# A 2-layer block on one core: the RWKV row stage, the recurrence and the layer's end get a new order of work

## The reference, cut to what matters

```python
r, k, v = jnp.einsum('nbtc,ncd->nbtd', xs[:3], w_rkv)
w_log = -jax.nn.softplus(-(w0 + jnp.tanh(xw @ w1) @ w2)) - 0.5
decay = jnp.exp(-jnp.exp(w_log))
a = jax.nn.sigmoid(a0 + (xa @ a1) @ a2)
g = jax.nn.sigmoid(xg @ g1) @ g2
kk = split(k * k_k)
kk = kk / jnp.maximum(jnp.sqrt(jnp.sum(kk * kk, axis=-1, keepdims=True)), 1e-12)
k_mod = k * (1.0 + (a - 1.0) * k_a)
# per head: S_t = S_{t-1} diag(w_t) + (S_{t-1} a_t) b_t^T + v_t k_t^T ;  y_t = S_t r_t
y = wkv7(rh, wh, kh, vh, -kk, kk * ah)
y = (y - mean) * lax.rsqrt(var + GN_EPS) * gn_g + gn_b        # per head
y = y + jnp.sum(rh * kh * r_k, axis=-1, keepdims=True) * vh   # the bonus
out = (y.reshape(B, T, C) * g) @ wo
```

## Time and profile before

| | |
|---|---|
| median of 3 runs | 1590.67 us (1590.26 to 1593.71) |
| the profiled execution | 1589.26 us, its span 1587.4 us |
| mean granted TensorE clock | 0.942 of 2.4 GHz |
| busy in the span | PE 90%, DVE 56%, ACT 44%, POOL 4% |

### The profile page before, as it was taken

How to read it: one execution, slowest core, us unless ns; L and a number is a source line. 1 busy time by engine, 2 the same in 40 slices (tenths; PEclk the granted TensorE clock), 3 DMA queues, 4 the chain that set the end, 5 groups by cost and what they waited for, 6 DMA issues and landing times.

```text
span 1587.4 us, 22472 instructions
## 1 busy us (share of the span) xinstructions
PE 1426.4 (90%) x8310; PEld 1164.7 (73%) x8310; DVE 883.2 (56%) x1246; ACT 703.2 (44%) x1125; POOL 68.3 (4%) x51
## 2 busy tenths in 40 slices
PE   6999999788979889999996798888999983899998
PEld 5888877666767778887874688857888862578887
DVE  4454567865533454455939654355555577355554
ACT  5343465453544453444444222224444463454443
POOL 0000000000000000000005003100000001000000
PEclk9999999888999999999898899969999996899999
DMA  8556556334434446465423000033555640135553
GB/s 267 185 180 210 169 163 212 106 120 146 133 105 160 123 157 213 159 196 188 134 67 118 2 3 28 19 106 117 189 184 185 201 160 27 53 123 184 192 182 113
DMA packets 145859, 221.43 MB, mean 139 GB/s; under 512 B 16844, under 2 KB 65240, under 8 KB 145656
## 3 DMA queue, kind: packets, MB, share of 16 engines
q1 hardware_dynamic: 145784, 220.40, 42.1%
HBM read 219.30 MB, written 1.05 MB: 139 GB/s over the span
## 4 chain that ended last, share of the span: by engine, by line
PE 81%; DVE 11%; ACT 5%; issue 2%; POOL 1%; DMA 1%; SPq 0%; ACTq 0%; DVEq 0%
PE acc L268 11%; PE gp L268 11%; PE acc L269 11%; PE acc L270 11%; PE gp L270 11%; PE gp L269 11%; PE tp L839 1%; DVE sb_w_lo L262 1%; PE gp L2116 1%; PE acc L2132 1%; ACT sb_arena L2604 1%; PE acc L2129 1%; PE tp L449 1%; ACT sb_xa_hi L427 1%; DVE sb_xa_lo L434 1%
## 5 line engine op out<-in xcount | busy, mean ns | idle before, releaser
L262 DVE TENSOR_TENSOR sb_w_lo<-sb_raw,sb_w_hi 128x1024 fp32r<-128x1024 f32 x400 | 479.3, 1228 | 252.5 <-ACT sb_w_hi L251 251.7
L251 ACT ACTIVATE sb_w_hi<-sb_raw 128x1024 fp32r<-128x1024 f32 x400 | 409.7, 1059 | 288.9 <-PE acc L270 150.6
L268 PE MATMUL gp<-sb_w_hi,sb_xa_hi 128*128 128x512 f32 (+1 forms) x736 | 295.8, 402 | 15.2 <-DVE sb_xa_lo L434 10.0
L270 PE MATMUL gp<-sb_w_lo,sb_xa_hi 128*128 128x512 f32 (+1 forms) x736 | 289.8, 394 | 0.0
L269 PE MATMUL gp<-sb_w_hi,sb_xa_lo 128*128 128x512 f32 (+1 forms) x736 | 289.6, 393 | 0.0
L268 PEld LDWEIGHTS gp<-sb_w_hi,sb_xa_hi 128*128 128x128 f32 x736 | 141.7, 193 | 49.7 <-issue 17.1
L270 PEld LDWEIGHTS gp<-sb_w_lo,sb_xa_hi 128*128 128x128 f32 x736 | 141.1, 192 | 30.0
L269 PEld LDWEIGHTS gp<-sb_w_hi,sb_xa_lo 128*128 128x128 f32 x736 | 141.8, 193 | 27.5
L268 PE MATMUL acc<-sb_w_hi,sb_mid_hi 128*128 128x512 f32 x408 | 159.1, 390 | 0.0
L270 PE MATMUL acc<-sb_w_lo,sb_mid_hi 128*128 128x512 f32 x408 | 158.9, 389 | 0.0
L269 PE MATMUL acc<-sb_w_hi,sb_mid_lo 128*128 128x512 f32 x408 | 158.7, 389 | 0.0
(11 more groups left out here) (371 smaller groups left out, 1848.2 us busy)
## 6 DMA issues: line engine op xcount, KB each, us to landing
sb_raw<-in_ffn_w SPq DMA_DIRECT2D x264, 256.0 KB, 4.3
sb_raw<-in_mlp_w SPq DMA_DIRECT2D x256, 256.0 KB, 2.9
sb_raw<-in_w_in SPq DMA_DIRECT2D x72, 256.0 KB, 3.5
sb_raw<-in_a_w_rkv SPq DMA_DIRECT2D x48, 256.0 KB, 3.6
sb_raw<-in_xattn_w_kv SPq DMA_DIRECT2D x32, 256.0 KB, 3.6
sb_raw<-in_w_out SPq DMA_DIRECT2D x16, 256.0 KB, 3.0
sb_raw<-in_xattn_w_q SPq DMA_DIRECT2D x16, 256.0 KB, 5.5
sb_raw<-in_xattn_w_o SPq DMA_DIRECT2D x16, 256.0 KB, 4.0
```

The costliest lines, as they stand in the source:

```text
L251: A.e.activation(w_hi[:, s], raw[:, r], ACT.Copy).then_inc(hi_done, 1)
L262: V.e.tensor_tensor(w_lo[:, s], raw[:, r], w_hi[:, s].bitcast(F32), ALU.subtract).then_inc(lo_done, 1)
L268: e.matmul(dst, xh, wh, start=start, stop=False)
L270: return e.matmul(dst, xh, wl, start=False, stop=stop)
```

## The change

- Biases: w0 and a0 become a 65th row of the second low-rank matrices, against a row of ones (read from the table `causal`), so the sigmoids read PSUM directly. The a parts move to `up_a` and `low_a`, in the memory of `mid`. k_k and k_a are loaded early, r_k after up-a.
- Order of TensorE: first half of k, g, up-w, second half of k (into `tp`), decay ends, up-a, first half of v, the sums, the sum shifted by one token as a product with the table `tri` moved by a column (`pe_sum`), token tile 0 of v's second half, the shifted sum of tile 1. Tile 1 of v's second half is done in four pieces within unit 0, whose transposes come alone.
- k*k_k, b, r and all of the head norm move from GpSimd to VectorE. GpSimd keeps the powers. kk is worked on by column halves.
- The bonus weights (`dve_weigh`) are made in iterations 1 and 2 of the recurrence, output chunks are split in iterations 1 to 4, and tile 0's norm and bonus run in iterations 5 to 7.
- Stream 1's buffers lie in the memory of `xb` and `mid`, so six output chunks are loaded before the recurrence.
- The last unit is interleaved with tile 0's gate, transposes (two groups of four k tiles, `pe_wide`) and its output product for the first 512 columns. Tile 1's norm is done in two parts, twelve heads and four. `pe_out` then does tile 1's gate, and the rest of the product by token and column half.

The diff, cut to its core and eight columns of indent taken off:

```diff
+    before = np.arange(-1, P)[None, :]
+    put("tri", -DECAY * ((s <= before).astype(np.float32) - (s < P // 2).astype(np.float32)))
...
+        mid_f = [shadow[:, x, :] for x in range(2)]
+        self.up_a, self.low_a, self.r_k = mid_f[0], mid_f[1][:, 0:256], mid_f[0]
...
+        sp.dma_start(self.up[64:65, :], a["a_w0_2"]).then_inc(self.lora2_loaded, 16)
+        sp.dma_start(self.low_w[64:65, :], self.ones()).then_inc(self.lora2_loaded, 16)
...
+        r, k, v = self.prods
+        for c in range(r.first[0], r.first[1]):
             load_chunk(sp, c)
-        self.bias(sp, 1, 0, a["a_w0_2"][0], xattn.post.freed)
-        self.bias(sp, 2, 1, a["a_a0_2"][0], ffn2_post.freed)
-        for c in range(self.prods[0].end, second):
+        sp.wait_ge(chunk_used, ffn2.end)
+        sp.dma_start(self.up_a[0:64, :], a["a_a2_2"][0]).then_inc(self.up_a_loaded, 16)
+        sp.dma_start(self.up_a[64:65, :], a["a_a0_2"]).then_inc(self.up_a_loaded, 16)
+        sp.dma_start(self.low_a[64:65, :], self.ones()).then_inc(self.up_a_loaded, 16)
+        for c in range(r.first[1], r.end):
             load_chunk(sp, c)
-        self.bias(sp, 3, 0, a["a_k_k_2"][0], (self.w_in, NT))
-        for c in range(second, self.prods[2].end):
+        sp.wait_ge(*ffn2_post.freed)
+        sp.dma_start(gain_b[1][:, :], a["a_k_k_2"][0].partition_broadcast(P)).then_inc(self.bias_loaded, 16)
+        for c in range(k.first[0], k.end):
...
+        sp.wait_ge(*xattn.post.freed)
+        sp.dma_start(gain_b[0][:, :], a["a_k_a_2"][0].partition_broadcast(P)).then_inc(self.k_a_loaded, 16)
+        for c in range(v.first[0], v.end):
+            load_chunk(sp, c)
+        sp.wait_ge(self.a_up, NT)
+        sp.wait_ge(self.bias_loaded, 16)
+        sp.dma_start(self.r_k, a["a_r_k_2"][0].rearrange("h d -> (h d)").partition_broadcast(P)).then_inc(self.bias_loaded, 16)
+        for c in range(self.out.first[0], self.out.first[0] + 6):
...
-        sp.wait_ge(self.y_done, 2 * self.GROUPS)
-        for c in range(ahead, self.out.end):
+        for c in range(self.out.first[0] + 6, self.out.end):
             load_chunk(sp, c)
...
-        self.pe_product(T, 0, XA, 4, (1,))
+        r, k, v = self.prods
+        r.pe(T, 1, XA, self.bank(1), (self.mixed_lo, 4))
         self.pe_wa(T)
-        self.pe_product(T, 1, XB, 5, (0, 1))
+        k.pe(T, 0, XB, self.bank(2), (self.mixed_lo, 5), stage(self.taken, 2))
...
+    def pe_sum(self, T, t, dst, tri, done):
+        for b in range(2):
+            mm = T.e.matmul(dst(b), tri, rows(0)[:, t, b * 512:(b + 1) * 512], start=True, stop=True)
+        mm.then_inc(*T.one(done))
...
-        T.e.wait_ge(self.lora2_loaded, 32)
-        T.e.wait_ge(self.low, 4)
+        r, k, v = self.prods
+        T.e.wait_ge(self.lora2_loaded, 48)
+        T.e.wait_ge(*stage(self.taken, 4))
+        self.pe_up_rows(T, self.low_w, self.up, self.w_up)
+        k.pe(T, 1, XB, self.bank(3), (self.mixed_lo, 5), (self.low, 4))
+        T.e.wait_ge(self.w_sig, NT)
         T.e.wait_ge(*stage(self.taken, 6))
-        self.pe_up_rows(T, 0, self.w_up)
-        self.prods[2].pe(T, 0, XA, self.bank(4), (self.mixed_lo, 6), stage(self.taken, 8))
-        T.e.wait_ge(self.w_in, NT)
-        self.pe_up_rows(T, 1, self.a_up)
-        self.prods[2].pe(T, 1, XA, self.bank(5), (self.mixed_lo, 6), stage(self.taken, 10))
-        T.e.wait_ge(self.a_in, NT)
-        T.e.wait_ge(self.w_sig, NT)
-        for t in range(NT):
-            for b in range(2):
-                mm = T.e.matmul(acc[:, t, b * 512:(b + 1) * 512], const("tri"), rows(0)[:, t, b * 512:(b + 1) * 512], start=True, stop=True)
-            mm.then_inc(*T.one(self.cum))
         for c in range(KT):
             for t in range(NT):
...
+        T.e.wait_ge(self.up_a_loaded, 48)
+        self.pe_up_rows(T, self.low_a, self.up_a, self.a_up)
+        v.pe(T, 0, XA, self.bank(4), (self.mixed_lo, 6), (self.low, 5))
+        for t in range(NT):
+            T.e.wait_ge(self.a_ready, t + 1)
+            self.pe_sum(T, t, lambda b: acc[:, t, b * 512:(b + 1) * 512], const("tri")[:, 1:P + 1], self.cum)
+        T.e.wait_ge(*stage(self.taken, 10))
+        self.pe_sum(T, 0, lambda b: gp[:, b, :], const("tri")[:, 0:P], self.prev)
+        self.pe_v_token(T, 0, range(0, 4)).then_inc(*T.one(self.v_half))
+        T.e.wait_ge(self.prev_exp, 1)
+        self.pe_sum(T, 1, lambda b: gp[:, b, :], const("tri")[:, 0:P], self.prev)
...
+        V.e.wait_ge(*V.last)
+        V.e.wait_ge(self.exp_c, t + 1)
+        V.e.tensor_tensor(rows(4)[:, t, :], rows(4)[:, t, :], rows(1)[:, t, :], ALU.mult).then_inc(*V.one())
+        V.e.tensor_tensor(rows(5)[:, t, :], rows(5)[:, t, :], gain_b[1 - t][:, :], ALU.mult).then_inc(*V.one())
+        V.e.tensor_tensor(rows(2)[:, t, :], rows(2)[:, t, :], gain_b[1 - t][:, :], ALU.mult).then_inc(*V.one())
+        V.e.wait_ge(self.prev_exp, t + 1)
+        V.e.scalar_tensor_tensor(rows(7)[:, t, :], rows(7)[:, t, :], -1.0, rows(0)[:, t, :], ALU.mult, ALU.mult).then_inc(*V.one(self.rows_ready))
...
+        r, k, v = self.prods
+        split_lo(V, k.end)
+        self.dve_kk_raw(V, 0)
+        self.dve_kk_ss(V, 0)
+        self.dve_kk_rows(V, 0)
+        split_lo(V, v.first[1])
+        self.dve_kk_raw(V, 1)
+        self.dve_kk_ss(V, 1)
+        self.dve_k_mod(V, 0)
+        self.dve_k_mod(V, 1)
+        split_lo(V, v.first[1] + 2)
+        self.dve_kk_rows(V, 1)
+        self.dve_b_rows(V, 0)
+        self.dve_b_rows(V, 1)
+        split_lo(V, v.end)
+        self.dve_scaled(V, 0)
+        self.dve_scaled(V, 1)
...
-        G.e.wait_ge(self.a_ready, NT)
-        for t in range(NT):
-            G.e.wait_ge(self.kk_rows, t + 1)
-            G.e.tensor_tensor(rows(2)[:, t, :], rows(7)[:, t, :], rows(1)[:, t, :], ALU.mult).then_inc(*G.one(self.b_rows))
-        G.e.wait_ge(self.bonus, NT)
-        for t in range(NT):
-            G.e.wait_ge(self.exp_c, t + 1)
-            G.e.tensor_tensor(rows(4)[:, t, :], rows(4)[:, t, :], rows(1)[:, t, :], ALU.mult).then_inc(*G.one(self.r_rows))
...
+        self.take_block(A, k, 0, 2, 5)
+        self.act_kk_squares(A, 0)
...
+        for t in range(NT):
+            A.e.wait_ge(self.w_up, t + 1)
+            A.e.activation(rows(0)[:, t, :], acc[:, t, :], ACT.Sigmoid).then_inc(*A.one(self.w_sig))
+        self.take_block(A, k, 1, 3, 5)
...
+        A.e.activation(self.decay_end, gp[:, 0, 0:KT], ACT.Copy).then_inc(*A.one(self.low))
+        self.act_kk_squares(A, 1)
+        A.e.wait_ge(self.kk_ss, 1)
+        for t in range(NT):
+            A.e.wait_ge(self.a_up, t + 1)
+            A.e.activation(rows(1)[:, t, :], acc[:, t, :], ACT.Sigmoid).then_inc(*A.one(self.a_ready))
+        self.take_block(A, v, 0, 4, 6)
+        self.act_decays(A, 0)
+        self.act_prev(A, 0)
+        self.act_decays(A, 1)
+        self.take_v_token(A, 0)
+        self.act_prev(A, 1)
+        A.e.wait_ge(*A.last)
+        A.e.activation(self.decay_end, self.decay_end, ACT.Exp).then_inc(*A.one(self.decay_ready))
...
+        else:
+            T.e.wait_ge(self.prev_exp, NT)
+            T.e.wait_ge(*stage(self.taken, 11 + s))
+        T.e.wait_ge(self.rows_ready, t + 1)
...
         self.pe_columns(T, 0)
+        self.pe_v_token(T, 1, range(0, 1))
+        self.pe_pairs(T, 0)
+        self.pe_v_token(T, 1, range(1, 2))
+        self.pe_a_mat(T, 0)
+        self.pe_v_token(T, 1, range(2, 3))
+        self.pe_z(T, 0, 0)
+        self.pe_v_token(T, 1, range(3, 4))
+        self.pe_xy(T, 0, 0)
+        self.pe_z(T, 0, 1)
+        self.pe_xy(T, 0, 1)
         self.pe_columns(T, 1)
...
+        y = rows(7)[:, 0, :]
+        self.pe_z(T, last, 3)
+        T.e.wait_ge(self.g2_loaded, 64)
+        T.e.wait_ge(self.y_done, last)
+        self.pe_gate(T, 0, 0)
+        self.pe_xy(T, last, 3)
+        self.pe_gate(T, 0, 1)
+        self.pe_z(T, last, 4)
+        self.turn.pe_wide(T, 0, 0, self.spare_bank(0), y, (self.y_rows, 1))
+        self.pe_xy(T, last, 4)
+        self.turn.pe_wide(T, 0, 1, self.spare_bank(1), y, (self.y_rows, 2))
+        self.pe_rhs(T, last)
+        self.pe_out_part(T, 0, 0, range(0, 1))
+        self.pe_u_first(T, last)
+        self.pe_out_part(T, 0, 0, range(1, 2))
+        self.pe_carry(T, last)
+        self.pe_out_part(T, 0, 0, range(2, 3))
+        self.pe_u_second(T, last)
+        self.pe_out_part(T, 0, 0, range(3, 4))
+        self.pe_y(T, last)
...
+            if u <= 3:
+                split_hi(A, self.out.first[0] + 2 * u - 1)
...
+            if u <= 3:
+                split_hi(A, self.out.first[0] + 2 * u)
+            if u == self.GROUPS + 1:
+                self.act_gn(A, 0)
+        last = self.UNITS - 1
+        self.act_z(A, last, 3)
+        self.act_z(A, last, 4)
+        self.act_gn(A, 1)
+        for g in range(2):
+            self.turn.act_wide(A, 0, g, self.spare_bank(g), XA)
+        self.act_rhs(A, last)
+        self.act_u(A, last, 0)
...
+        V.e.wait_ge(self.bias_loaded, 32)
+        V.e.wait_ge(*V.last)
```

(90 more changed lines are left out.)

522 lines of the change are left out of this document (253 added, 269 removed).

## The result

The changed kernel takes 1553.89 us (median of 4 runs, 1551.44 to 1557.22), the kernel before 1590.47 on the same chip: a ratio of 0.977, 95% interval [0.9745, 0.9794]. The prediction was 1548, range 1541 to 1560. The profiled execution took 1551.44, span 1549.4, so the spans differ by 38.0 us where the sum of the prediction said 42.4.

A forecast was written before the change was run, and what follows sets the result against it. TensorE, busy 90% of the span, was taken as the bound; 20.2 + 0.1 + 2.2 + 19.9 = 42.4 us off 1589.3 gave 1546.9, with 1.4 for the median 1548. Range 1543 to 1554, with rivals 1 to 4 1541 to 1560.

The forecast's parts named there:

- The row stage: From k's first half to unit 0's transposes: set by TensorE, 54.2 us instead of 74.4, 20.2 less.
- The first unit: Unit 0 with v's pieces of tile 1 inside it: 15.7 us instead of 15.76, 0.1 less.
- The recurrence: Units with 25 us of VectorE inserts placed in its waits, old inserts removed: 2.2 us less in sum.
- the two old inserts: Recurrence, ahead of the level-3 copies, 1.4 us each: removing them saves 2.5 us each, 5.0 in all.
- the weigh units: Two recurrence units in which VectorE makes the bonus weights: 0.15 us longer each.
- the three second-tile units: Recurrence units with VectorE's inserted norm and bonus operations of tile 0: 0.4 us longer for the three.
- rival 5: Recurrence: VectorE's inserts don't fit, 42 us longer there, v pieces uncovered, whole slower at 1594 us; chance 0.03.
- Last unit and output: Last unit interleaved with gates, transposes and output product: 42.9 us instead of 62.8, 19.9 less.
- Rival 1: The clock drops in the interleaved stage of last unit and output, eight us lost: 1556 us; chance 0.13.
- Rival 2: VectorE stays the end of the row stage, 5 us late at the far bound: 1553 us; chance 0.07.
- Rival 3: Behind the output product, the next layer's splits wait for slots, at most 5.45 us given back: 1553; chance 0.07.
- Rival 4: In one second-tile unit GpSimd's power holds VectorE, 3.1 us and about 1.2 of clock: 1552 us; chance 0.04.

The follow-up runs named there:

- decay spread: Changed kernel with the 16 one-column decay matmuls spread between the pieces of k's second half instead of in one block: median 1549.54 us, ratio 0.9737.
- shift on VectorE: Changed kernel with the shifted sum as two VectorE operations instead of four TensorE matmuls, ScalarE's exponentials behind it: ratio 0.9741.
- three edits: Changed kernel with decay columns spread, ScalarE's rounding behind y, and shifted sum on VectorE behind the exponentials: median 1544.14 us, ratio 0.9712.
- two rows late: Kernel with the three edits, plus two VectorE products for token tile 1's scaled rows moved behind unit 0's first copies: median 1543.95 us, ratio 0.9703.
- exponential late: Kernel with two rows late, plus tile 1's shifted exponential and the decay columns' exponential behind ScalarE's copies of unit 0's transposes: median 1546.85 us, ratio 0.971.

## Why the prediction was right, and where it was off

**The row stage.** Forecast 54.2, measured 57.9. That it ends on TensorE was right: busy 56.80 of 57.92 us, VectorE 4.3 us early with token tile 0's rows where 4.5 was forecast, and 7.4 us more put on it there changed nothing. (Its wait ahead of these rows is 4.63 us; by the prediction's own times it was 2.7, from 845 to 847.7.) The sum of TensorE's terms missed one thing: each was priced at the full clock. The decay columns cost 4.0 for 3.6, the up-projection behind them 7.2 for 3.6, v's first half 11.75 for 10.9. The two behind the columns ran at half the clock for some 9 us. These make 4.9 us, and spreading the columns gave back 4.9. Without them the sum would have been 1 us too long. The row for the columns in the earlier trace rows stood in a stretch where TensorE then waited, so it could not show what follows them. The part of the gain that comes from GpSimd's contention, argued from four rows, was shown by itself: 3.9 us, net of the 7.4 us that VectorE took over.

**The first unit.** Forecast 15.7, measured 17.0. I took v's pieces to cost 1.4 and 0.9, 2.3 in all; they cost 1.8. What was mis-sized is the unit without them: 15.2 by the experiment, with a clock of 0.89 (10.87 us busy, so some 1.2 us of it the clock's), where 13.4 was left in the sum. Why the unit is longer than the sum of its parts beyond that stays open.

**The recurrence.** Forecast 2.2 less, measured 3.3 less. ScalarE's rounding cost 0.6 a unit in three units, 1.8 (forecast 2.1), shown by taking it out. What was mis-sized is the price of the two old inserts: iterations 5 and 6, 20.4 us before, take 17.5 each with the new inserts, 2.9 less and not 2.5, 5.8 in all for 5.0. VectorE's 25 us of inserts cost nearly nothing: these two are as long as an iteration of the kernel before that had none (17.44), and the weigh units take as long without them as with them (118.34 and 118.36 over the seven), where I had 0.15 each. Only the last iteration is longer, 16.64 against 16.25: the 0.4 that the sum had for the three second-tile units together. That the waits of the earlier trace rows hold them is right, and rival 5 is out.

**Last unit and output.** Forecast 42.9, measured 43.0, and it was the interleaving and the clock as forecast: without it 54.7. The allowance of 1.0 for a lower clock was not used (1.00 in both rows), the work was 1 us longer; that the two cancel is luck.

**The rivals.** Rival 1 did not come in the stage where I had put it. A lower clock stood in the row stage, behind the decay columns, and in two of the experiments (decay spread, shift on VectorE) the clock was 0.92 in the 22 us ahead of the last unit, where the kernel after has 1.00 with the same code; that cost 2.0 to 2.3 us there, and why it fell stays open. Rival 2 is out by VectorE's wait. Rival 3 is out: 505.3 us behind the output product, 504.8 before. Rival 4 is out, for VectorE was not held. The power at 976.30 has VectorE's operation of 976.13 beside it, and the power at 830.85 has the one of 832.93; both have two SBUF inputs, and they took 1.22 and 1.23 us. The Trainium skill, in the section that the prediction named ("SBUF — State Buffer", "Who interferes with whom"), lets the order of issue decide who waits. The first pair agrees: VectorE's operation had begun 0.17 us earlier, and GpSimd's took 3.80 us instead of 2.90. The second does not: GpSimd's had begun 2.1 us earlier, and still VectorE's took 1.23. So far as these rows go, the measurement decides: a power of 128x16 did not hold VectorE. For wide operations the experiment that took them from GpSimd agrees with the section.

The whole came to 1553.9 for 1548: 3.7 us of it are the row stage, 1.3 the first unit, 1.1 back from the recurrence, and the median of the four runs lies 2.5 above the profiled execution, where 1.4 had been allowed; the stages behind the output product, 0.5 longer, make most of what is left.

## What to carry to other kernels

Add up an engine's queue at the full clock only where it has wide work throughout: 4 us of one-column matmuls looked busy, and the 9 us behind them ran at half the clock. Spread such a block between wide matmuls. Before work is moved to another engine, ask which of the two sets the end after all the other edits: the shifted sum went to TensorE just when that became the bound. And where several queues meet, write down for each what stands ahead of the first instruction that the next stage needs: the last microsecond of the three edits was in ScalarE's order, not in VectorE's length.

## What the runs showed of the hardware

The code ahead of the row stage is the same in the eleven kernels of the table, yet the first up-projection starts between 806.05 and 815.32 us. Busy time of the two extremes from 400 to 500 us, first the kernel with two rows late, then the one with the exponential late, both run on one and the same chip:

```profile
400.00:500.00 100.00, 88.00 (x395) 71.55 (x393) 47.43 (x64) 49.18 (x82) 4.43 (x6) 0.97 0.45 153
```

```profile
400.00:500.00 100.00, 88.00 (x380) 71.30 (x380) 45.25 (x62) 48.17 (x81) 4.43 (x6) 0.93 0.44 145
```

The granted clock differs by 0.04 for the same code, and over the first 400 us by 0.02 (0.96 and 0.94). By these figures the second kernel spent some 24 us more of the 500 at half the clock, which is an estimate of 11 us lost where 9.3 were measured. So up to 9 us of a run's time are the clock of the code ahead, as much as the three edits won; what sets it stays open. And some 4 us of one-column matmuls, with no idle time in the records, are followed by 1.2 GHz: 7.2 us for what takes 3.6 at 2.4 GHz.
